# The convolution computed with tokens on partitions, later block moves, and all moves of the mixer on ScalarE's queue

## The chip, the cores and the metric

The kernel runs on one core of a Trainium2 chip, in float32. The metric is the device time of one execution, in microseconds (us). An execution under the profiler gives the trace; other executions give the times.

## The reference

One layer of a hybrid encoder, on x of 256 tokens by 2048:

```
h  = rms_norm(x);  P = h @ W_in        # 2048 x 4416: u | b | c (1024 each), c_q 768, c_kv 512, k_rope 64
yA = b * dwconv3_causal(c * u)         # three taps per channel, over tokens
yA = group_rms_norm(yA, 8 groups of 128 channels)
q  = rms_norm(c_q) @ W_uq;  kv = rms_norm(c_kv) @ W_ukv
yB = attention of 8 heads (nope 128, rope 64, v 128), block-causal in chunks of 64; per-head rms_norm
x  = x + rms_norm(concat(yA, yB) @ W_o)
x  = x + rms_norm(relu(rms_norm(x) @ W_up)^2 @ W_down)     # hidden width 8192
```

## The kernel before, in words

**Products.** Every weight matrix is streamed once from DRAM in quads: four blocks of 128 rows by up to 512 columns, 1 MB, one DMA each on SyncE's queue (SP), into a ring of 4 slots (`raw`, L605). For each half of a quad, ScalarE rounds it to a high part (L1005, `w_hi`) and VectorE subtracts to get a low part (L1305, `w_lo`). TensorE forms each product from three matmuls, hi*hi, lo*hi and hi*lo (L725 to L727), for two blocks of 128 tokens. So a half of a quad is twelve matmuls. The hi/lo ring holds four halves (`AHEAD`): ScalarE may split half h + 4 once TensorE has finished half h.

**Order.** `plan()` (L76) writes one list of steps, and every engine walks that same list in order, doing its own part of each step. An instruction that waits therefore holds back everything behind it on its engine. A step `mm` (quad, k) is one fourth of a quad on TensorE; at every odd k ScalarE and VectorE split the half that lies four further on. First come three strips of the latent columns (halves 0 to 23; the third strip is only 320 columns wide), then six strips of u, c, b, u, c, b (512 columns each, `CONV_PARTS`), then the output projection from W_o, then the MLP. A counter `sub` numbers the `mm` steps of those six strips and of W_o: strips are steps 0 to 95, W_o starts at step 96. `between(sub)` puts the mixer's other work into the list before step `sub`. In this text "step 34" is `sub` 34.

**Attention.** The head pairs p = 0 to 3 start at step 8 + 16p. Relative to that start: k and q leave PSUM, `kq_turn` at 6 (VectorE transposes 32x32 blocks into `blk`), `q_order` at 13 (ScalarE copies the moved q into `qT`, L1138), `scores` at 15 (TensorE, L909), softmax, `pv` at 22, `o_squares` at 24 (VectorE reduces, GpSimd raises to -1/2), `o_norm` at 25, `o_turn` at 26, `o_split` at 36.

**Block moves.** A turned batch in `blk` has its blocks transposed in place, but they still have to change partitions. SyncE does this in `move_batch` (L624): it waits for the turn, writes four DMAs of `blk` to a DRAM scratch `mix_rows` (L634), waits until they have landed, and reads it back with one DMA (L647). It does this between weight loads, once quad n + 4 has been requested. There are twelve such batches: two of the latents, four kq, four o, two conv.

**Convolution.** The products c*u and b of the first 512 channels are turned and moved like the others (`conv_turn` at steps 38 and 54); those of the second 512 are transposed by TensorE (`convT`, L944, four calls of four transposes). The convolution then runs with channels on partitions, on 128x256 pieces, eight in all: ScalarE applies one tap, VectorE the other two (L1520) and b. ScalarE squares, a TensorE matmul against `ones` sums over partitions (L957, eight of them), ScalarE takes the root (L1200), VectorE inverts it (L1532), applies it and writes the hi and lo parts (L1533 to L1536). These are at steps 70 + 6c and following for the first half, 98 + 4c for the second.

**Residual.** At quad `RESIDUAL_QUAD` SyncE also loads `g_post_mix` and `x_res` (L680, L681).

Of the kernel before, what the change touches and what calls it, by code (L numbers as in the profile page):

```python
# [33 lines left out]
P = 128  # L34
# [32 lines left out]
G_MIX, G_MLP, G_Q, G_KV, G_CONV, G_ATT, G_TAP = 0, 16, 32, 38, 42, 50, 58  # L67
G_ROWS = G_TAP + 3 * (CW // P)
# [4 lines left out]
CONV_PARTS = "ucb" * 2  # L73


def plan():  # L76
# [53 lines left out]
    def between(sub):  # L130
        if sub == 2:
            steps.append(("latT", 0, 0))
# [4 lines left out]
        if sub in (38, 54):  # L137
            turn("conv", sub // 54)
        for p in range(PAIRS):
# [10 lines left out]
            if at == 6:  # L150
                turn("kq", p)
            if at == 26:
                turn("o", p)
# [5 lines left out]
        for c in range(4):  # L159
            for half, t, norm in [(0, 70 + 6 * c, 8), (1, 98 + 4 * c, 5)]:  # L160
                if sub == t:
                    steps.append(("convT", half, c))
                if sub == t + 2:
                    steps.append(("conv_square", half, c))
                if sub == t + norm:
                    steps.append(("conv_norm", half, c))
# [15 lines left out]
    order = [(0, 2), (0, 3), (0, 0), (1, 2), (1, 3), (1, 0), (0, 1), (1, 1)]  # L182
# [119 lines left out]
def hybrid_block(nc, t, out):  # L302
    steps, tail, quads, batches = plan()
    BATCH = {(kind, i): n for n, (kind, i, _) in enumerate(batches)}
# [6 lines left out]
    with ExitStack() as ctx:  # L311
# [10 lines left out]
        neg_half = tensor(ctx, "neg_half", [P, 4])  # L322
# [18 lines left out]
        mean_sq = tensor(ctx, "mean_sq", [P, 8, 4])  # L341
        eps_col = tensor(ctx, "eps_col", [P, 1])
# [10 lines left out]
        with ExitStack() as mixer:  # L353
# [4 lines left out]
            rotated = tensor(mixer, "rotated", [P, TB, 2, ROPE])  # L358
            cos_t = tensor(mixer, "cos_t", [P, TB, 2 * ROPE])
            sin_t = tensor(mixer, "sin_t", [P, TB, 2 * ROPE])  # L360
            rope_c = tensor(mixer, "rope_c", [P, 2, ROPE])
            rope_s = tensor(mixer, "rope_s", [P, 2, ROPE])
# [14 lines left out]
            NCONV = 2  # L377
            conv_y = tensor(mixer, "conv_y", [P, NCONV, SEQ])
            conv_s = tensor(mixer, "conv_s", [P, NCONV, SEQ])
            conv_u = tensor(mixer, "conv_u", [P, NCONV, SEQ])  # L380
# [48 lines left out]
        convT_filled, tap_ready, conv_y_ready = sem("convT_filled"), sem("tap_ready"), sem("conv_y_ready")  # L429
        conv_sq_ready, conv_sum_done = sem("conv_sq_ready"), sem("conv_sum_done")  # L430
        conv_std_ready = sem("conv_std_ready")
# [80 lines left out]
        mix_rows = nc.dram_tensor("mix_rows", (4, BLK, 4, 8 * BLK), F32, kind="Internal").ap()  # L512
# [13 lines left out]
        def conv_landed(e):  # L526

            return as_blocks((u_sb, b_sb)[e][:, 0].rearrange("p b n -> p (b n)"))
# [52 lines left out]
        def conv_blocks(e, c):  # L581

            return conv_landed(e)[:, :, :, c].rearrange("p g b i -> p b g i")
# [3 lines left out]

        def conv_bank(half, c):
            return 7 if half == 0 else 4 + c
# [12 lines left out]
        def _(sp):  # L602
# [21 lines left out]
            def move_batch(m):  # L624

                kind, i, _ = batches[m]
                size = 4 * BLK if kind == "o" else 8 * BLK
                sp.wait_ge(blk_turned, m + 1)
                if m:

                    sp.wait_ge(blk_landed, 16 * m)
                for g in range(4):
                    src = blk[BLK * g:BLK * (g + 1)].rearrange("p q b c i -> p q (b c i)")[:, :, 0:size]
                    sp.dma_start(mix_rows[:, :, g, 0:size].rearrange("q r n -> r q n"), src).then_inc(blk_stored, 16)  # L634
                if kind == "kq":
                    sp.wait_ge(latT_lo_ready, 2)
                    if i:
                        sp.wait_ge(scores_done, 2 * i)
                elif kind == "lat" and i:
                    sp.wait_ge(latT_lo_ready, i)  # L640
                elif kind == "o":
                    sp.wait_ge(latT_lo_ready, 3)
                    sp.wait_ge(kr_ready, 4)
                    if i:
                        sp.wait_ge(oT_lo_ready, i)
                sp.wait_ge(blk_stored, 64 * (m + 1))
                sp.dma_start(landing(kind, i), mix_rows[:, :, :, 0:size].rearrange("q r g n -> (q r) g n")  # L647
                             ).then_inc(blk_landed, 16)

# [13 lines left out]
            for n in range(RAW, NQ):  # L663
# [6 lines left out]
                if n == 7:  # L670
                    sp.dma_start(ident[:], t["ident"]).then_inc(ident_landed, 16)
                    sp.dma_start(cos_t[:], t["cos"]).then_inc(tables_landed, 16)
                    sp.dma_start(sin_t[:], t["sin"]).then_inc(tables_landed, 16)
                for m, (_, _, after) in enumerate(batches):
                    if after == n:
                        move_batch(m)
                if n == RESIDUAL_QUAD:

                    sp.wait_ge(oT_lo_ready, PAIRS)
                    sp.dma_start(g_post_mix[:], t["post_mix_g"].to_broadcast([P, D])).then_inc(g_mix_landed, 16)  # L680
                    sp.dma_start(x_res[:], x_dram).then_inc(x_res_landed, 16)  # L681
# [36 lines left out]
        def _(pe):  # L718
# [50 lines left out]
            def stream(n, k, tbs=range(TB)):  # L769
# [103 lines left out]
            def step(what, a, b):  # L873
# [61 lines left out]
                elif what == "convT" and a == 1:  # L935

                    pe.wait_ge(strip_out_dve, 2)
                    pe.wait_ge(strip_out_act, 7)

                    pe.wait_ge(o_ready, PAIRS)  # L940
                    if conv_bank(a, b) == conv_bank(0, 0):

                        pe.wait_ge(conv_std_ready, 4)
                    transposes(conv_bank(a, b), [s[:, a, tb, b * P:(b + 1) * P] for s in (u_sb, b_sb)  # L944
                                                 for tb in range(TB)]).then_inc(convT_filled, 1)
                elif what == "conv_norm":

                    i = 4 * a + b
                    pe.wait_ge(ones_ready, 1)
                    pe.wait_ge(conv_sq_ready, i + 1)  # L950
                    if i == 0:

                        pe.wait_ge(probsT1_ready, PAIRS)
                    elif a == 0:

                        pe.wait_ge(conv_std_ready, b)
                    nc.tensor.matmul(ps[:, conv_bank(a, b), 0:SEQ], ones[:], conv_s[:, i % NCONV, :],  # L957
                                     start=True, stop=True).then_inc(conv_sum_done, 1)
# [39 lines left out]
        def _(act):  # L998
# [58 lines left out]
            def step(what, a, b):  # L1057
# [116 lines left out]
                elif what == "convT":  # L1174
                    i = 4 * a + b
                    if a:
                        act.wait_ge(convT_filled, b + 1)
                    else:
                        act.wait_ge(blk_landed, landed(("conv", 1)))
                    if i >= NCONV:  # L1180

                        act.wait_ge(convT_ready, i - NCONV + 1)

                    tap = G_TAP + 2 * 8 + i
                    if a:
                        nc.scalar.activation(conv_y[:, i % NCONV], ps[:, conv_bank(a, b), 0:SEQ], ACT.Copy,
                                             scale=gains[:, tap:tap + 1]).then_inc(tap_ready, 1)
                    else:
                        nc.scalar.activation(by_block(conv_u[:, i % NCONV]), conv_blocks(0, b), ACT.Copy)
                        nc.scalar.activation(by_block(conv_y[:, i % NCONV]), conv_blocks(0, b), ACT.Copy,  # L1190
                                             scale=gains[:, tap:tap + 1]).then_inc(tap_ready, 1)
                elif what == "conv_square":
                    i = 4 * a + b
                    act.wait_ge(conv_y_ready, i + 1)
                    nc.scalar.activation(conv_s[:, i % NCONV], conv_y[:, i % NCONV],
# [636 lines left out]
```

## Time and profile before

| | us |
|---|---|
| median of 3 runs | 1068.28 (1066.87 to 1068.4) |
| the profiled execution's own time | 1067.39 |
| span of its trace, from the first to the last instruction | 1065.6 |
| TensorE busy | 1053.6 |
| VectorE busy | 695.2 |
| ScalarE busy | 515.9 |
| GpSimd busy | 80.7 |

Lines name the engines PE (TensorE matmul), PEld (its weight load), DVE (VectorE), ACT (ScalarE), POOL (GpSimd) and SP (SyncE); a "q" behind the name is that engine's sequencer, as where it issues a DMA. Busy times are sums over the span. A matmul's end is modelled, so the distance between the starts of two matmuls, not the length of one, tells what one costs.

### The profile page before, as it was taken

What the parts mean: (1) busy time and instruction counts of PE and PEld (TensorE: products, weight loads), DVE (VectorE), ACT (ScalarE), POOL (GpSimd) and SP (SyncE); (2) the same over time, 40 slices, a digit from 0 to 9 for tenths busy, and PEclk for the clock granted to TensorE, in tenths of its full rate; (3) what the DMA queues carried; (4) which work ended last, traced back from release to release, by engine and by line L of the source; (5) the groups of instructions that cost most, each with busy time, mean ns of one, the idle gap of its engine ahead of it and who ended that gap; (6) DMA issues with size and microseconds to landing.
All of it is one profiled execution on the core that took longest, in us unless ns stands there. A gap on an engine that the chain in (4) does not pass through costs nothing.

```text
span 1065.6 us, 13494 instructions
## 1 busy us (share of the span) xinstructions
PE 1053.6 (99%) x4794; PEld 877.0 (82%) x4794; DVE 695.2 (65%) x785; ACT 515.9 (48%) x666; POOL 80.7 (8%) x94
## 2 busy tenths in 40 slices
PE   9999999999999999999999999999999999999996
PEld 7898888888888788888888888888888888888885
DVE  6475566679975876575575665756657656565666
ACT  7575545565544664444444444444444444444443
POOL 0011022110000310000000000000000000000003
PEclk9999999999999999999999999999999999999998
DMA  9786667864586465776666756666576665676562
GB/s 345 261 300 218 201 184 272 271 221 151 204 307 198 125 212 157 237 226 197 209 184 212 231 172 232 196 199 212 170 236 216 203 211 159 220 232 190 181 242 79
DMA packets 125619, 225.78 MB, mean 212 GB/s; under 512 B 8464, under 2 KB 30096, under 8 KB 124816
## 3 DMA queue, kind: packets, MB, share of 16 engines
q1 hardware_dynamic: 125152, 224.89, 64.7%
q10 hardware_dynamic: 432, 0.44, 0.1%
q8 instruction: 21, 0.34, 0.1%
q14 instruction: 14, 0.11, 0.0%
HBM read 210.08 MB, written 7.34 MB: 204 GB/s over the span
## 4 chain that ended last, share of the span: by engine, by line
PE 85%; issue 11%; DVE 2%; POOL 1%; DMA 1%; ACT 0%; SPq 0%; DVEq 0%; POOLq 0%; ACTq 0%
PE ps L725 28%; PE ps L727 28%; PE ps L726 28%; DMA raw<-in_w_in 1%; PE ps L748 1%; POOL acc L1666 0%; DVE w_lo L1305 0%; PE ps L909 0%; PE ps L914 0%; POOL x_res L1777 0%; POOL x_res L1751 0%; ACT w_hi L1005 0%; SPq L656 0%; DVE conv_s L1532 0%; DVEq L311 0%
## 5 line engine op out<-in xcount | busy, mean ns | idle before, releaser
L1305 DVE TENSOR_TENSOR w_lo<-raw,w_hi 128x1024 fp32r<-128x1024 f32 (+2 forms) x382 | 465.2, 1226 | 318.9 <-ACT w_hi L1005 316.8
L1005 ACT ACTIVATE w_hi<-raw 128x1024 fp32r<-128x1024 f32 (+2 forms) x382 | 395.8, 1038 | 460.7 <-PE ps L727 456.3
L725 PE MATMUL ps<-w_hi,xT_hi 128*128 128x512 f32 (+1 forms) x792 | 308.5, 390 | 0.6 <-DVE xT_lo L1406 0.5
L727 PE MATMUL ps<-w_lo,xT_hi 128*128 128x512 f32 (+1 forms) x792 | 305.9, 386 | 0.0
L726 PE MATMUL ps<-w_hi,xT_lo 128*128 128x512 f32 (+1 forms) x792 | 305.8, 386 | 0.0
L725 PE MATMUL ps<-w_hi,yT_hi 128*128 128x512 f32 x672 | 263.1, 391 | 0.0
L727 PE MATMUL ps<-w_lo,yT_hi 128*128 128x512 f32 x672 | 261.6, 389 | 0.0
L726 PE MATMUL ps<-w_hi,yT_lo 128*128 128x512 f32 x672 | 261.4, 389 | 0.0
L725 PEld LDWEIGHTS ps<-w_hi,xT_hi 128*128 128x128 f32 x792 | 148.7, 188 | 31.9 <-issue 2.0
L727 PEld LDWEIGHTS ps<-w_lo,xT_hi 128*128 128x128 f32 x792 | 148.6, 188 | 30.0
L726 PEld LDWEIGHTS ps<-w_hi,xT_lo 128*128 128x128 f32 x792 | 148.8, 188 | 28.7
L727 PEld LDWEIGHTS ps<-w_lo,yT_hi 128*128 128x128 f32 x672 | 126.1, 188 | 26.5
L726 PEld LDWEIGHTS ps<-w_hi,yT_lo 128*128 128x128 f32 x672 | 126.2, 188 | 26.1
L725 PEld LDWEIGHTS ps<-w_hi,yT_hi 128*128 128x128 f32 x672 | 126.1, 188 | 25.9
L1379 DVE TENSOR_TENSOR acc<-acc,ps 128x1024 f32<-128x1024 f32 x58 | 70.8, 1220 | 18.4 <-PE ps L727 17.5
L1685 POOL TENSOR_TENSOR a_sb<-a_sb 128x1024 f32<-128x1024 f32 x16 | 30.3, 1895 | 583.0 <-ACT a_sb L1035 583.0
L1035 ACT ACTIVATE a_sb<-ps,rstd_x 128x512 f32<-128x512 f32 x32 | 20.2, 683 | 19.9 <-PE ps L727 19.9
L1325 DVE TENSOR_TENSOR yT_lo<-aT_raw,yT_hi 128x512 fp32r<-128x512 f32 x32 | 20.6, 683 | 0.0
L1350 DVE STREAM_TRANSPOSE a_blk<-a_sb 128x512 f32<-128x512 f32 x30 | 19.5, 687 | 0.0
L1044 ACT ACTIVATE yT_hi<-aT_raw 128x512 fp32r<-128x512 f32 x32 | 18.2, 615 | 1.5 <-DVE aT_raw L1360 1.5
L1672 POOL TENSOR_TENSOR rope_c<-q_sb,cos_t 128x128 f32<-128x128 f32 x8 | 8.6, 1073 | 114.6 <-ACT q_sb L1129 114.3
L727 PE MATMUL ps<-w_lo,cqT_hi 128*128 128x384 f32 x48 | 16.1, 335 | 0.0
(155 smaller groups left out, 425.3 us busy)
## 6 DMA issues: line engine op xcount, KB each, us to landing
raw<-in_w_up SPq DMA_DIRECT2D x64, 1024.0 KB, 5.5
raw<-in_w_down SPq DMA_DIRECT2D x64, 1024.0 KB, 5.3
raw<-in_w_in SPq DMA_DIRECT2D x28, 1024.0 KB, 6.0
raw<-in_w_o SPq DMA_DIRECT2D x16, 1024.0 KB, 5.0
aT_raw<-a_blk SPq DMA_DIRECT2D x240, 32.0 KB, 1.9
raw<-in_w_uq SPq DMA_DIRECT2D x8, 576.0 KB, 4.9
mix_rows<-blk SPq DMA_DIRECT2D x32, 128.0 KB, 2.4
raw<-in_w_ukv SPq DMA_DIRECT2D x4, 1024.0 KB, 5.3
```

The source lines that it names most:

```text
L725: nc.tensor.matmul(dst, x_hi, hi, start=first, stop=False)
L726: nc.tensor.matmul(dst, x_lo, hi, start=False, stop=False)
L727: mm = nc.tensor.matmul(dst, x_hi, lo, start=False, stop=last)
L748: mm = nc.tensor.transpose(ps[:, bank, i * P:(i + 1) * P], src, ident[:])
L1005: nc.scalar.activation(w_hi[:, slot, 0:size], raw[:, raw_slot, first:first + size], ACT.Copy).then_inc(hi_ready, 1)
L1035: ins = nc.scalar.activation(a_sb[:, tb], ps[:, bank + tb], ACT.Relu, scale=rstd_x2[:, tb:tb + 1])
L1044: ins = nc.scalar.activation(turned(yT_hi, at, tb), blocked(tb), ACT.Copy)
L1305: nc.vector.tensor_tensor(w_lo[:, slot, 0:size], raw[:, raw_slot, first:first + size], f32(w_hi[:, slot, 0:size]), ALU.subtract).then_inc( ...
L1325: ins = nc.vector.tensor_tensor(turned(yT_lo, at, tb), blocked(tb), f32(turned(yT_hi, at, tb)), ALU.subtract)
L1350: ins = nc.vector.transpose(a_blk[:, :, tb].rearrange("p q c i -> p c q i"), a_sb[:, tb].rearrange("p (c q i) -> p c q i", c=4, q=4))
L1379: nc.vector.tensor_tensor(m, m, ps[:, bank:bank + 2], ALU.add).then_inc(acc_added, 1)
L1685: nc.gpsimd.tensor_tensor(a, a, a, ALU.mult).then_inc(a_ready, 1)
```

## The change

1. The convolution stays with tokens on partitions. The product c*u (256 x 512 of a half) is stored to a second DRAM scratch `conv_rows` with two zero rows ahead of it, and read back twice, shifted by one and two tokens (`u_store`, `u_back1`, `u_back2`, ScalarE's queue). The taps are loaded as rows broadcast to all partitions (`taps`). VectorE does six operations on 128x1024 (`conv_mix` 0 to 5), ScalarE one square, VectorE one reduction, GpSimd the power -1/2, VectorE one scaling; then both halves are turned and moved as blocks (`conv_turn`) and split by both engines (`conv_split`). TensorE's transposes (`convT`) and its sums against `ones` are gone.
2. Steps: the turns of conv are at 89 and 104 instead of 38 and 54; the splits at 105 and 115.
3. All twelve moves are issued by ScalarE (`move_store`, `move_read`). The store is in the list one step after the turn, and the read 4 (kq), 5 (o) or 6 (conv) steps after it. `mix_rows` has two halves, used in turns.
4. W_o's first two strips take row block 0 later: (0,2) (0,3) (1,2) (1,3) (0,0) (1,0) (0,1) (1,1).
5. `x_res` is loaded four quads after `g_post_mix`, and `g_post_mix` also waits for `ss_c_ready`.

```diff
-    def turn(kind, i):
-        batches.append((kind, i, len(quads) + 4))
+    def turn(kind, i, at=None):
+        batches.append((kind, i))
         steps.append((kind + "_turn", i, len(batches) - 1))
+        if at is not None:
+            moves.setdefault(at + 1, []).append(("move_store", len(batches) - 1, 0))
+            moves.setdefault(at + MOVE[kind], []).append(("move_read", len(batches) - 1, 0))
...
+                for b, when in enumerate([((1, 2, 3), (1, 3, 3)), ((2, 0, 3), (2, 2, 2))]):
+                    if (s, q, k) in when:
+                        steps.append((("move_store", "move_read")[when.index((s, q, k))], b, 0))
...
     def between(sub):
+        steps.extend(moves.pop(sub, []))
...
-        if sub in (38, 54):
-            turn("conv", sub // 54)
...
             if at == 6:
-                turn("kq", p)
+                turn("kq", p, sub)
             if at == 26:
-                turn("o", p)
+                turn("o", p, sub)
...
+        for h in range(2):
+            for when, what in [(4, "taps"), (34, "u_store"), (40, "u_back1"), (67, "u_back2")] if h == 0 else [
+                    (79, "taps"), (83, "u_store"), (88, "u_back1"), (88, "u_back2")]:
+                if sub == when:
+                    steps.append((what, h, 0))
+            for op, when in enumerate([(50, 56, 58, 76, 77, 83), (87, 91, 92, 94, 95, 98)][h]):
+                if sub == when:
+                    steps.append(("conv_mix", h, op))
+            for when, what in [[(84, "conv_square"), (86, "conv_stats"), (89, "conv_scale"), (105, "conv_split")],
+                               [(99, "conv_square"), (101, "conv_stats"), (104, "conv_scale"), (115, "conv_split")]][h]:
+                if sub == when:
+                    steps.append((what, h, 0))
+            if sub == (89, 104)[h]:
+                turn("conv", h, sub)
...
-            def move_batch(m):
...
+                if n == 9:
+                    sp.wait_ge(zeros_ready, 1)
+                    sp.dma_start(conv_rows[:, 0:2].rearrange("h r n -> r h n"),
+                                 blk[0:2].rearrange("p q b c i -> p (q b c i)").rearrange("p (h n) -> p h n", h=2)
+                                 ).then_inc(zeros_stored, 16)
...
-                            pe.wait_ge(convT_ready, 4 * z["q"] + 4)
+                            pe.wait_ge(convT_ready, z["q"] + 1)
...
+                elif what == "move_store":
+                    kind, i = batches[a]
+                    size = 4 * BLK if kind == "o" else 8 * BLK
+                    act.wait_ge(blk_turned, a + 1)
+                    for g in range(4):
+                        src = blk[BLK * g:BLK * (g + 1)].rearrange("p q b c i -> p q (b c i)")[:, :, 0:size]
+                        act.dma_start(mix_rows[a % 2, :, :, g, 0:size].rearrange("q r n -> r q n"), src
+                                      ).then_inc(blk_stored, 16)
+                elif what == "move_read":
...
+                    act.wait_ge(blk_stored, 64 * (a + 1))
+                    act.dma_start(landing(kind, i), mix_rows[a % 2, :, :, :, 0:size].rearrange("q r g n -> (q r) g n")
+                                  ).then_inc(blk_landed, 16)
...
+                elif what == "conv_split":
+                    act.wait_ge(blk_landed, landed(("conv", a)))
+                    for c in range(4):
+                        k = 4 * a + c
+                        ins = nc.scalar.activation(by_block(yT_hi[:, k]),
+                                                   conv_landed(a)[:, :, :, c].rearrange("p g b i -> p b g i"),
+                                                   ACT.Copy, scale=gains[:, G_CONV + k:G_CONV + k + 1])
+                    ins.then_inc(convT_hi_ready, 1)
...
+                elif what == "conv_mix":
+                    u = u_sb[:, a]
+                    dst, other, op = [(u, tap(2), ALU.mult), (shifted[0], tap(1), ALU.mult), (u, shifted[0], ALU.add),
+                                      (shifted[1], tap(0), ALU.mult), (u, shifted[1], ALU.add),
+                                      (u, b_sb[:, a], ALU.mult)][b]
...
+                    nc.vector.tensor_tensor(dst, dst, other, op).then_inc(conv_mixed, 1)
```

## Rows read from the trace of the kernel before

**Rows 1.** The page: busy time of each engine, share of the span, instructions.
```profile
PE 1053.6 (99%) x4794; PEld 877.0 (82%) x4794; DVE 695.2 (65%) x785; ACT 515.9 (48%) x666; POOL 80.7 (8%) x94
```

**Rows 2.** TensorE's waits from 15 to 1045 us: total, times, longest.
```profile
PE ps L748 <- POOL x_res L1751: 0.5, 1, 0.5
```

**Rows 3.** Busy time in a stretch: length, then busy (count) of each engine, clock, DMA.
```profile
247.00:300.00 53.00, 53.00 (x243) 43.76 (x242) 50.70 (x71) 27.67 (x41) 0.81 (x1) 1.00 0.64 223
```

**Rows 4.** Timeline of TensorE (start, length, engine, line) around a transpose and a sum.
```profile
272.41 0.39 PE L727 MATMUL ps<-w_lo,yT_hi 128*128 128x512 f32 x1
273.31 0.39 PE L726 MATMUL ps<-w_hi,yT_lo 128*128 128x512 f32 x1
...
274.23 0.39 PE L727 MATMUL ps<-w_lo,yT_hi 128*128 128x512 f32 x1
275.11 0.39 PE L726 MATMUL ps<-w_hi,yT_lo 128*128 128x512 f32 x1
```

**Rows 5.** Timeline of TensorE: the scores of pairs 1, 2 and 3.
```profile
147.24 1.47 PE L909 MATMUL ps<-kqT,lat 128*128 128x128 f32 x8
...
185.44 1.47 PE L909 MATMUL ps<-kqT,lat 128*128 128x128 f32 x8
...
223.65 1.47 PE L909 MATMUL ps<-kqT,lat 128*128 128x128 f32 x8
```

**Rows 6.** Timeline of VectorE around pair 1's turn of kq and pair 0's of o.
```profile
137.26 0.67 DVE L1334 STREAM_TRANSPOSE blk<-q_sb 128x512 f32<-128x512 f32 x1
138.75 1.23 DVE L1305 TENSOR_TENSOR w_lo<-raw,w_hi 128x1024 fp32r<-128x1024 f32 x1 [0.83 <-ACT w_hi L1005]
...
143.31 0.69 DVE L1502 TENSOR_TENSOR o_sb<-o_sb,rstd_o 128x512 f32<-128x512 f32 x1 [1.42 <-POOL rstd_o L1658]
...
145.38 0.70 DVE L1334 STREAM_TRANSPOSE blk<-o_sb 128x512 f32<-128x512 f32 x1
```

**Rows 7.** Timeline of ScalarE in the same stretch.
```profile
137.66 1.06 ACT L1005 ACTIVATE w_hi<-raw 128x1024 fp32r<-128x1024 f32 x1 [3.02 <-PE ps L727]
...
143.35 1.06 ACT L1005 ACTIVATE w_hi<-raw 128x1024 fp32r<-128x1024 f32 x1 [1.66 <-PE ps L727]
145.14 0.72 ACT L1138 ACTIVATE lat<-kqT 128x256 f32<-128x256 f32 x2 [0.72 <-DMA kqT<-mix_rows]
```

**Rows 8.** Timelines of SyncE's and ScalarE's queues: issues of a move, and one on ScalarE.
```profile
137.95 1.78 SPq L634 DMA_DIRECT2D mix_rows<-blk  x4
141.71 0.34 SPq L647 DMA_DIRECT2D kqT<-mix_rows  x1
...
1.18 0.45 ACTq L1050 DMA_DIRECT2D xT_raw<-in_xT  x1
```

**Rows 9.** Timeline of VectorE: the turns of o of pairs 1 and 2.
```profile
182.28 0.70 DVE L1334 STREAM_TRANSPOSE blk<-o_sb 128x512 f32<-128x512 f32 x1
...
220.48 0.70 DVE L1334 STREAM_TRANSPOSE blk<-o_sb 128x512 f32<-128x512 f32 x1
```

**Rows 10.** Timelines of ScalarE, VectorE and TensorE in the last latent strip.
```profile
55.99 1.70 ACT L1106 ACTIVATE cqT_hi<-kqT,gains 128x256 fp32r<-128x256 f32 x4
...
54.44 1.30 DVE L1334 STREAM_TRANSPOSE blk<-lat 128x512 f32<-128x512 f32 x2
...
57.72 2.19 DVE L1339 SCALAR_TENSOR_TENSOR cqT_lo<-kqT,gains,cqT_hi 128x128 fp32r<-128x128 f32 x8 [0.78 <-ACT cqT_hi L1106]
...
61.21 0.31 PE L726 MATMUL ps<-w_hi,xT_lo 128*128 128x320 f32 x1
```

**Rows 11.** All DMAs that touch the scratch: issue to landing.
```profile
DMA to landing us min/median/max: 1.7/2.7/6.3
```

**Rows 12.** Timelines of TensorE and ScalarE: two neighbouring matmuls, and a table load.
```profile
248.98 0.39 PE L726 MATMUL ps<-w_hi,xT_lo 128*128 128x512 f32 x1
249.21 0.39 PE L727 MATMUL ps<-w_lo,xT_hi 128*128 128x512 f32 x1
...
237.53 1.28 ACT L1200 ACT_TABLE_LOAD   x1
```

More of the change, by code:

```diff
@@ L179, in plan @@
         steps.append(("conv_out", i, n))
-    order = [(0, 2), (0, 3), (0, 0), (1, 2), (1, 3), (1, 0), (0, 1), (1, 1)]
+    order = [(s, q) for qs in ((2, 3), (0,), (1,)) for s in (0, 1) for q in qs]
     order += [(s, q) for s in (2, 3) for q in (2, 3, 0, 1)]
@@ L622, in move_blocks @@
                                      ).then_inc(aT_landed, 16)
-            def move_batch(m):
[L626 to L648, printed above, removed]
             def load_x(tb):
@@ L934, in step @@
                     mm.then_inc(pv_done, 1)
[L935 to L958, printed above, removed]
                 elif what == "hT":
@@ L1173, in step @@
                                rstd_x).then_inc(strip_out_act, 1)
-                elif what == "convT":
-                    i = 4 * a + b
-                    if a:
-                        act.wait_ge(convT_filled, b + 1)
-                    else:
[L1179 to L1191, printed above, removed]
-                elif what == "conv_square":
-                    i = 4 * a + b
-                    act.wait_ge(conv_y_ready, i + 1)
-                    nc.scalar.activation(conv_s[:, i % NCONV], conv_y[:, i % NCONV],
-                                         ACT.Square).then_inc(conv_sq_ready, 1)
-                elif what == "conv_norm":
-                    i = 4 * a + b
-                    act.wait_ge(conv_sum_done, i + 1)
-                    nc.scalar.activation(conv_s[:, i % NCONV], ps[:, conv_bank(a, b), 0:SEQ], ACT.Sqrt,
-                                         scale=1.0 / P, bias=eps_col[:, 0:1]).then_inc(conv_std_ready, 1)
@@ new lines, in step @@
+                elif what == "move_store":
[7 more added lines that the diff above has]
+                elif what == "move_read":
+                    kind, i = batches[a]
+                    size = 4 * BLK if kind == "o" else 8 * BLK
+                    if kind == "kq":
+                        act.wait_ge(latT_lo_ready, 2)
+                        if i:
+                            act.wait_ge(scores_done, 2 * i)
+                    elif kind == "lat" and i:
+                        act.wait_ge(latT_lo_ready, i)
+                    elif kind == "o":
+                        act.wait_ge(latT_lo_ready, 3)
+                        act.wait_ge(kr_ready, 4)
+                        if i:
+                            act.wait_ge(oT_lo_ready, i)
+                    if a:
+                        act.wait_ge(blk_landed, 16 * a)
+                    act.wait_ge(blk_stored, 64 * (a + 1))
+                    act.dma_start(landing(kind, i), mix_rows[a % 2, :, :, :, 0:size].rearrange("q r g n -> (q r) g n")
+                                  ).then_inc(blk_landed, 16)
+                elif what == "taps":
+                    if a:
+                        act.wait_ge(conv_mixed, 4)
+                    for k in range(3):
+                        act.dma_start(conv_w[:, k], t["conv_w"][0, k:k + 1, a * W:(a + 1) * W].to_broadcast([P, W])
+                                      ).then_inc(conv_w_landed, 16)
+                elif what == "u_store":
+                    act.wait_ge(strip_out_dve, a + 1)
+                    act.dma_start(conv_rows[a, 2:2 + SEQ].rearrange("(b p) n -> p b n", p=P), u_sb[:, a]
+                                  ).then_inc(u_stored, 16)
+                elif what in ("u_back1", "u_back2"):
+                    back = int(what[-1])
+                    act.wait_ge(u_stored, 16 * (a + 1))
+                    act.wait_ge(zeros_stored, 16)
+                    if a:
+                        act.wait_ge(ss_c_ready, a)
+                    elif back == 1:
+                        act.wait_ge(latT_lo_ready, 3)
+                        act.wait_ge(krT_filled, 1)
+                    else:
+                        act.wait_ge(q_rope_ready, 4 * PAIRS)
+                        act.wait_ge(qrT_filled, PAIRS)
+                    act.dma_start(shifted[back - 1], conv_rows[a, 2 - back:2 - back + SEQ].rearrange(
+                        "(b p) n -> p b n", p=P)).then_inc(u_shifted[back - 1], 16)
+                elif what == "conv_square":
+                    act.wait_ge(conv_mixed, 6 * a + 6)
+                    nc.scalar.activation(shifted[0], u_sb[:, a], ACT.Square).then_inc(conv_sq_ready, 1)
+                    if a == 0:
+                        nc.scalar.activation(std_m[:], ones[:, 0:TB], ACT.Sqrt)
+                elif what == "conv_split":
[6 more added lines that the diff above has]
+                    ins.then_inc(convT_hi_ready, 1)
@@ L1423, in step @@
                 elif what == "conv_turn":
-                    if a == 0:
-                        dve.wait_ge(strip_out_dve, 1)
-                    else:
-                        dve.wait_ge(strip_out_act, 5)
-                    src = (u_sb, b_sb)[a]
-                    turn_batch(b, [src[:, 0, tb].rearrange("p (c q i) -> p c q i", c=4, q=4) for tb in range(TB)])
+                    dve.wait_ge(conv_scaled, a + 1)
+                    turn_batch(b, [u_sb[:, a, tb].rearrange("p (c q i) -> p c q i", c=4, q=4) for tb in range(TB)])
                 elif what == "lat_split":
```

131 lines of the change are left out of this document (67 added, 64 removed).

## The prediction, made before the changed kernel had run

> **What bounds the kernel now.** I read the busy times first [rows 1]: TensorE works 1053.6 of the span's 1065.6 us, no other engine more than two thirds of it. Then who waits on TensorE's side [rows 2]: between 15 and 1045 us it waited 0.5 us in all. So each matmul taken out shortens the kernel by its own cost, and each microsecond for which TensorE has to wait lengthens it. An engine beside it costs nothing until it is later than the ring of four halves allows. Two neighbouring matmuls start 0.23 us apart [rows 12], so a half (twelve) passes in about 2.72 us and a step in 1.36. VectorE is the engine closest to being late: in the convolution's stretch it is busy 50.7 of 53 us [rows 3].
>
> **What TensorE sheds.** From a product to the next but one takes 0.90 us with a group of four transposes in between, and 0.88 us with a sum against `ones` [rows 4]; two plain distances are 0.46. So a group of transposes costs 0.44 and a sum 0.42 us. There are four groups and eight sums: 4 x 0.44 + 8 x 0.42 = 5.1 us. All of it is on the path, since TensorE never rests there.
>
> **Other work that goes, comes or moves, and is hidden.** The weight loads leave SyncE earlier, as no move stands between them any more; since TensorE does not wait for loads now [rows 2], that is worth 0. The zero rows (8 KB) go out with quad 9, long before the first turn needs `blk`: 0. The loads of taps and the shifts by DRAM have 4 to 27 steps each before their users: 0 to 1 us. The new order of W_o's quads only gives the convolution more time. `g_post_mix` and `x_res` are needed tens of microseconds later: 0.
>
> **The moves on ScalarE: attention.** This is the part that decides. SyncE could wait for a turn without hurting anyone; ScalarE has the hi splits and `q_order` queued behind the waiting store. A store is four issues, 1.78 us on SyncE, and one issue on ScalarE's queue took 0.45 [rows 8], so I take 1.77 us per store; from below, if they overlap other work, 1.2.
>
> Pair 1, on before's clock. The turn of kq ends at 137.26 + 0.67 = 137.93 [rows 6]. ScalarE would start its next split at 137.66 [rows 7], but the store (step 31) stands ahead of it and waits for the turn: 137.93 + 1.77 = 139.70. The split is 2.0 us late, so VectorE's part of it (138.75 [rows 6]) is too, and behind that on VectorE come the reduction, GpSimd's power, `o_norm` (143.31) and the turn of pair 0's o, which ended at 145.38 + 0.70 = 146.08 [rows 6] and now ends at 148.1. At step 35 the store of this o waits on ScalarE for exactly that turn: 148.1 + 1.77 = 149.9. Behind it come the split of step 35 (1.06, at 143.35 before) and only then `q_order` (0.72, at 145.14 before) [rows 7]: 151.6. TensorE reaches the scores at 147.24 [rows 5] and needs `qT`. Wait: 4.4 us.
>
> Pair 2 has no product c*u on VectorE in the chain; before, its turn of o ended at 182.98 [rows 9]. 182.98 + 2.05 + 1.77 + 1.06 + 0.72 = 188.6 against 185.44 [rows 5]: 3.1 us. Pair 3: 220.48 + 0.70 = 221.18 [rows 9], the same terms and one more issue (`u_back2`, 0.43): 227.2 against 223.65 [rows 5]: 3.6 us. Pair 0 has no store of o ahead of its `q_order`; the read goes out about when it did: 0 (at most 2.4, below). Together 11.1 us. From below, without the 2.0 us of lateness and with stores of 1.2 us: 1.8 + 0.5 + 0.9, about 3 us.
>
> **The latents.** The narrow third strip leaves little time. The second turn (54.44 + 1.30 before [rows 10]) becomes about 1.0 us later since the read of the first batch, which waits for its stores, stands before ScalarE's output of the second strip. The second store (step after that turn) then waits until 56.7 and issues until 58.5; `lat_split` follows (1.70), at 55.99 before [rows 10], now 58.5 to 60.2; VectorE's part (2.19 [rows 10]) ends at 62.4 and the lo split behind it at 63.2. TensorE wants that half at 61.2 [rows 10]. Wait: 2.0 us (0.5 to 4).
>
> **The convolution's new place.** From step 83 to 104 VectorE has 11 lo splits and 7 mixes of 128x1024, 2 reductions and 2 scalings of the same size, 4 turns of 128x512 and the split of pair 3's o: 22 x 1.15 + 4 x 0.63 + 1.1 = 28.9 us (a 1024-wide operation is 1.23 long, a turn 0.70 [rows 6], and neighbours overlap by 0.08). TensorE passes these 22 steps in 29.9 us. That would fit, but VectorE also waits for others there: for ScalarE while it issues the store of pair 3's o and `u_store` (2.2 us), while it squares and loads the root's table (1.06 + 1.28 [rows 12]), 0.7 at the store of conv 0, 2.1 at the second square, 1.2 for GpSimd's power. 28.9 + 8.5 = 37.4 against 29.9 and some 3.5 us in hand: TensorE waits about 4 us, in pieces at several halves. Then one chain at steps 104 and 105: scale and turn (2.4), the store on ScalarE (1.77), `conv_split` of the first half on ScalarE (4 pieces, 1.7 as in [rows 10]) and on VectorE (2.1, [rows 10]), and only then the lo split of that step (1.15): 9.1 us from the moment at which VectorE gets to the scaling. I find that moment 4.5 us before TensorE wants step 112's half and `convT_ready`: 4.6 us more. The second half has five steps to spare: 0. Together 8.7 us; from below, if VectorE finds gaps that I count as waits, 2; from above 14.
>
> **Sum.** -5.1 + 11.1 + 2.0 + 8.7 = +16.7 us. From the profiled execution's own 1067.4 us this gives 1084; the median of the runs shown is 0.9 higher, so I say 1085.
>
> **A rule weighed.** The moves now share the 16 DMA engines with weight loads from another queue, instead of standing in line with them. Before, a DMA of the scratch landed 2.7 us after its issue, at most 6.3 [rows 11]. The Trainium skill (DMA: Bandwidth & Descriptors, "Issuing engines are not separate DMA queues") says that DMAs started by several engines run on the same 16 engines and interleave, and that a second issuer saves only issue time, usually small. By it no transfer gets quicker, which agrees with my 0 for the loads; taken as "issue time is small" it would also make the stores on ScalarE nearly free, and the sum would drop by the eight stores of 1.77 that stand in it, about 14 us, to 1070, the upper end of the absorbed case below; the row of 1.78 us speaks against that [rows 8].
>
> **The rivals.**
> - *Waits mostly absorbed*: the same mechanism at its lower ends: -5.1 + 3 + 0.5 + 2 = about 0, or 1068; with the latents at 2 and the convolution at 5 us +5, or 1072. I put the case at 1071. For it: ScalarE is busy only 48% and each engine has slack of several us in the ring. Against it: the order of the list is fixed, and `q_order` cannot pass the store.
> - *TensorE's work alone decides* (the other side): no wait reaches it, for which the turns would have to end some 4 us earlier against the scores than the rows show. 1067.4 - 5.1 = 1062. It decides where `q_order` ends before TensorE gets to the scores in all four pairs. For it: ScalarE has 52% idle time and VectorE is busy 65% [rows 1], so each has room on the whole. Against it: rows 5 to 9.
> - *Moves land late*: with reads or stores at 6.3 instead of 2.7 to 3.3 [rows 11], pair 0's `q_order` is 2.4 us late, the latents 3 more, the second conv move 3: +8 on the forecast, 1093. For it: the loads no longer leave a gap for the moves. Against it: a 512 KB read with a load just behind it took 3.4 us before.
> - *The change does nothing that can be told*: gains and waits cancel, within 0.2% (2 us, about what a measurement can tell from no change): 1068.
>
> **How the numbers follow.** Forecast 0.60; absorbed 0.15 (a third of it within 0.2% or just above); late landings 0.15; TensorE alone 0.06; cancelled 0.04. The range reaches from the absorbed case, 1071, to the late landings, 1095. Faster by over 0.2%: 0.07; within: 0.05; slower: 0.88.
>
> **What would show each step.** In the changed trace: no `ones` sums and no transposes of `u_sb`; TensorE idle before the scores of pairs 1, 2 and 3 by 3 to 4.5 us each, released by ScalarE's `q_order`, and none before pair 0's; ScalarE's stores of o issued right after VectorE's turn; idle of about 2 us near 61 us behind VectorE's lo split; several waits of under 1 us behind lo splits in steps 88 to 104 and one of over 4 at step 112. I am wrong if TensorE has no idle before the scores, if a store on ScalarE takes well under 1 us, or if VectorE reaches step 104 more than 9 us ahead of TensorE's step 112.

## The result and the profile after

The changed kernel takes 1100.13 us (median of 4 runs, 1098.55 to 1101.99) against 1067.91 on the same chip (1066.87 to 1068.4): ratio 1.0303, 95% interval 1.029 to 1.0316. So it is 32 us slower. I had said 1085, range 1071 to 1095: the direction was right, the size was not. The profiled execution has a span of 1096.8 us at a granted clock of 0.988, against 1065.6 at 0.997.

First the page of the changed kernel: busy times, and the clock in 40 slices. It answers to [rows 1].

```profile
PE 1059.2 (97%) x4762; PEld 877.5 (80%) x4762; DVE 686.2 (63%) x761; ACT 508.6 (46%) x649; POOL 88.7 (8%) x98
...
PEclk9999999999989999999999999999999999999998
```

TensorE has 32 matmul instructions fewer and is busy 5.6 us longer. Two things are to be seen in that: work went, and what is left runs slower somewhere. Slice 12, from 302 to 329 us, is the only one in the middle with a lower clock digit. VectorE and ScalarE do less than before, and so no engine has become the bound; the time is in waits. The view of waits on TensorE (total, times, longest), where [rows 2] had the 0.5 us of `x_res` alone:

```profile
PE ps L716 <- DVE w_lo L1313: 13.8, 7, 6.0
PE ps L900 <- issue: 11.7, 3, 4.6
PE ps L849 <- POOL ones L1704: 1.9, 1, 1.9
...
PE ps L739 <- POOL x_res L1773: 0.5, 1, 0.5
```

"Issue" as the releaser of the scores (L900) means only that the profile shows nothing that TensorE waited for. What did is told by ScalarE's timeline around pair 1's scores. Its columns are start, length, engine, line, operation; "ACTq" is an issue on ScalarE's queue.

```profile
144.49 1.78 ACTq L1147 DMA_DIRECT2D mix_rows<-blk  x4
146.37 2.01 ACT L972 ACTIVATE w_hi<-raw 128x1024 fp32r<-128x1024 f32 x2 [5.19 <-issue]
...
154.83 1.81 ACTq L1147 DMA_DIRECT2D mix_rows<-blk  x4
156.75 1.06 ACT L972 ACTIVATE w_hi<-raw 128x1024 fp32r<-128x1024 f32 x1 [8.37 <-DMA mix_rows<-blk]
157.71 0.70 ACT L1105 ACTIVATE lat<-kqT 128x256 f32<-128x256 f32 x2
```

and VectorE's in the same stretch, which answers to [rows 6]:

```profile
143.79 0.67 DVE L1344 STREAM_TRANSPOSE blk<-q_sb 128x512 f32<-128x512 f32 x1
147.47 1.22 DVE L1313 TENSOR_TENSOR w_lo<-raw,w_hi 128x1024 fp32r<-128x1024 f32 x1 [3.00 <-ACT w_hi L972]
...
154.10 0.70 DVE L1344 STREAM_TRANSPOSE blk<-o_sb 128x512 f32<-128x512 f32 x1
```

The turn of o ends at 154.80 and the store is issued from 154.83 on, the very moment. Behind it come the split and `q_order` (L1105), whose last piece ends at 158.41. TensorE starts the scores at 158.52:

```profile
158.52 2.30 PE L900 MATMUL ps<-kqT,lat 128*128 128x128 f32 x8 [4.59 <-issue]
160.75 1.65 PE L905 MATMUL ps<-krT,qrT_sb 64*128 64x128 f32 x8
...
201.79 1.55 PE L900 MATMUL ps<-kqT,lat 128*128 128x128 f32 x8 [3.25 <-issue]
203.27 0.93 PE L905 MATMUL ps<-krT,qrT_sb 64*128 64x128 f32 x8
...
244.11 2.55 PE L900 MATMUL ps<-kqT,lat 128*128 128x128 f32 x8 [3.88 <-issue]
246.59 1.55 PE L905 MATMUL ps<-krT,qrT_sb 64*128 64x128 f32 x8
```

Read the lengths as well as the pauses. The same eight matmul instructions of scores and eight of the rotated part take 2.41 us from first start to last end in pair 2 (201.79 to 204.20), but 3.88 in pair 1 and 4.03 in pair 3. The view by windows (start:end, length, busy time of PE, PEld, DVE, ACT, POOL, then the granted clock, DMA share, GB/s) says why:

```profile
60.00:64.00 4.00, 3.88 (x16) 3.88 (x17) 2.11 (x4) 2.45 (x7) 0.00 (x0) 0.57 0.49 119
...
158.00:163.00 5.00, 4.48 (x18) 3.02 (x19) 2.78 (x6) 1.36 (x3) 0.00 (x0) 0.66 0.64 213
201.00:205.00 4.00, 3.21 (x20) 2.39 (x21) 3.15 (x6) 1.64 (x4) 0.00 (x0) 1.00 0.49 135
244.00:249.00 5.00, 4.89 (x20) 3.42 (x21) 2.63 (x6) 0.95 (x2) 0.00 (x0) 0.66 0.90 290
288.00:293.00 5.00, 4.59 (x13) 3.62 (x14) 4.08 (x8) 3.68 (x6) 0.00 (x0) 0.66 0.58 161
...
318.00:324.00 6.00, 5.43 (x15) 4.33 (x16) 3.92 (x4) 1.27 (x2) 0.00 (x0) 0.58 0.52 183
```

After five of the larger pauses, TensorE ran for some microseconds on the lower level (1.2 GHz) before the granted clock was back at 2.4. After pair 2's it did not. Nor did it after the pause of 2.42 us at 68 us. The cost can be read off the starts of matmuls, here at the biggest pause:

```profile
312.22 0.39 PE L718 MATMUL ps<-w_lo,yT_hi 128*128 128x512 f32 x1
318.57 0.80 PE L716 MATMUL ps<-w_hi,yT_hi 128*128 128x512 f32 x1 [5.96 <-DVE w_lo L1313]
319.16 0.63 PE L717 MATMUL ps<-w_hi,yT_lo 128*128 128x512 f32 x1
319.58 0.63 PE L718 MATMUL ps<-w_lo,yT_hi 128*128 128x512 f32 x1
...
323.00 0.40 PE L717 MATMUL ps<-w_hi,yT_lo 128*128 128x512 f32 x1
323.24 0.40 PE L718 MATMUL ps<-w_lo,yT_hi 128*128 128x512 f32 x1
```

Neighbours are 0.43 apart instead of the 0.23 of [rows 12]. Eleven distances (318.57 to 323.24) take 4.67 us where 11 x 0.227 = 2.50 would do: 2.2 us lost. The same sum gives 1.6 us from 60.12 to 63.48, 1.7 from 288.41 to 292.41, and the scores 1.5 and 1.6: 8.6 us in all.

**The account.** The pauses of 0.15 us and more before the latents, the scores and the tail of the convolution add up to 2.31 + 2.42, 4.59 + 3.25 + 3.88 and 0.15 + 0.41 + 0.34 + 2.19 + 5.96 = 25.5 us. By distances of starts they are some 0.16 longer each (6.35 - 0.23 = 6.12 for the one shown as 5.96): 27.1. With the lower clock 8.6, and 5.1 for the matmuls that went, the sum is 27.1 + 8.6 - 5.1 = +30.6 us; the spans differ by 31.2. So 0.6 us has no place. The kernel's start does not fill it: GpSimd clears `blk` first and lets TensorE begin at 1.86 us instead of 1.01, but a wait of 0.88 us for a hi split a little later is gone, and the first matmul of L716 starts at 12.43 us, where its like (L725) started at 12.77 before, so 0.3 us earlier. With that, some 0.9 us is open.

### The profile page after: what moved, and what is told of

It reads as the page before. It is cut to its first block, busy times and chain, and to the rows that moved or that the text cites. A ratio compares the mean times of both kernels' runs of the same rounds, so it can differ in the third digit from the quotient of the medians.

```text
span 1096.8 us, 13395 instructions
## 1 busy us (share of the span) xinstructions
PE 1059.2 (97%) x4762; PEld 877.5 (80%) x4762; DVE 686.2 (63%) x761; ACT 508.6 (46%) x649; POOL 88.7 (8%) x98
## 4 chain that ended last, share of the span: by engine, by line
PE 79%; issue 10%; DVE 3%; DMA 3%; POOL 2%; ACT 2%; ACTq 1%; SPq 0%; DVEq 0%; POOLq 0%
PE ps L716 26%; PE ps L718 26%; PE ps L717 26%; DMA raw<-in_w_in 2%; DVE w_lo L1313 1%; DMA mix_rows<-blk 1%; ACT w_hi L972 1%; PE ps L900 1%; ACTq L1147 1%; PE ps L739 1%; POOL acc L1682 0%; POOL rstd_c L1674 0%; PE ps L905 0%; DVE u_sb L1537 0%; DVE blk L1344 0%
## 5 line engine op out<-in xcount | busy, mean ns | idle before, releaser
L716 PE MATMUL ps<-w_hi,xT_hi 128*128 128x512 f32 (+1 forms) x792 | 309.5, 391 | 6.2 <-DVE w_lo L1313 5.6
L716 PE MATMUL ps<-w_hi,yT_hi 128*128 128x512 f32 x672 | 263.7, 392 | 8.2 <-DVE w_lo L1313 8.1
L716 PEld LDWEIGHTS ps<-w_hi,xT_hi 128*128 128x128 f32 x792 | 149.5, 189 | 39.7 <-DVE w_lo L1313 8.5
L716 PEld LDWEIGHTS ps<-w_hi,yT_hi 128*128 128x128 f32 x672 | 127.1, 189 | 36.1 <-DVE w_lo L1313 9.7
L900 PE MATMUL ps<-kqT,lat 128*128 128x128 f32 (+1 forms) x32 | 7.9, 401 | 11.7 <-issue 11.7
L1688 POOL TENSOR_TENSOR rope<-q_sb,rope 128x128 f32<-128x128 f32 x8 | 8.6, 1073 | 120.2 <-ACT q_sb L1096 119.9
```

What stands on the lines that cost most here:

```text
L716: nc.tensor.matmul(dst, x_hi, hi, start=first, stop=False)
L900: nc.tensor.matmul(ps[:, (6, 7)[h], cols], qT[:, tb, h], kT, start=tb == 0, stop=False, skip_group_check=True)
```

## The experiments

Eight kernels, each timed beside the kernel before on the same chip (1067.5 to 1067.6 us).

**1. All moves back on SyncE, the convolution as changed.**

```diff
-            moves.setdefault(at + 1, []).append(("move_store", len(batches) - 1, 0))
-            moves.setdefault(at + MOVE[kind], []).append(("move_read", len(batches) - 1, 0))
+            pass
...
+                for m, (_, _, after) in enumerate(batches):
+                    if after == n:
+                        move_batch(m)
```

> The changed kernel, but all twelve moves back on SyncE's queue, where they stood before (after quad n + 4 has been requested); the convolution, its steps and the two halves of the scratch stay. Theory (ScalarE in order: what is queued behind a store that waits for its turn is late): TensorE's pauses before the scores of pairs 1 to 3 (12 us), the two in the third latent strip (5) and the half-clock stretches behind three of them (4.9) go, and the tail's pauses shrink as no store stands ahead of the hi splits there: 1100 - 22 = 1078 or less. Rival (the convolution's own work on VectorE makes the kernel slow, wherever the moves are issued): the pauses before the scores stay above 1 us each and the time stays above 1090. Rival (the pauses come from slow landings, since moves and loads share the DMA engines): on SyncE the same bytes move, so the pauses stay.

Measured: 1070.08 us, ratio 1.0019 [1.0009, 1.003], lower than the 1078 that I had named as the most. 30 of the 32 us are gone with this one edit. TensorE's waits in it:

```profile
PE ps L744 <- DVE w_lo L1341: 4.5, 3, 2.2
PE ps L877 <- POOL ones L1732: 1.9, 1, 1.9
...
PE ps L928 <- issue: 0.2, 1, 0.2
```

The scores wait 0.2 us in all instead of 11.7, the latents not at all; three pauses of the convolution's tail stay (1.75, 0.52 and 2.25 us). The loads of weights stand in one queue with the moves again and nothing waits for them.

**2. The kernel before, with nothing changed but the moves: ScalarE's queue, two halves of the scratch.**

```diff
+MOVE = {"kq": 4, "o": 5, "conv": 6}
...
-                for m, (_, _, after) in enumerate(batches):
-                    if after == n:
-                        move_batch(m)
...
+                elif what == "move_store":
```

> The kernel before, with only the moves put on ScalarE's queue, with the same distances to their turns (store one step later, read 4, 5 or 6 steps after the turn). Theory: the pauses of the latents and of the scores come as in the changed kernel, 17 us and about 5 us at half clock, and none at step 112: 1068 + 22 = 1090. If the moves were harmless and the new convolution the cause, 1068 within 2 us.

Measured: 1092.62 us, ratio 1.0227 [1.021, 1.0244]: 25 us for the moves alone, with TensorE's work untouched. Its waits:

```profile
PE ps L890 <- issue: 11.1, 3, 4.6
PE ps L706 <- DVE w_lo L1314: 5.6, 4, 3.5
PE ps L717 <- ACT w_hi L1047: 1.4, 1, 1.4
```

The three pauses before the scores are those of the changed kernel (4.56, 3.25, 3.33 against 4.59, 3.25, 3.88). Experiments 1 and 2 together say that the moves carry the loss, from either side: taken out of the changed kernel they give back 30 us, put into the old one they cost 25. The 5 us between the two belong to neither alone: the pauses of the convolution's tail are 9.1 us with both, 4.5 in experiment 1 and 0.9 here.

**3. Only the store of o later: four steps after its turn instead of one, behind `q_order`.**

```diff
-            moves.setdefault(at + 1, []).append(("move_store", len(batches) - 1, 0))
-            moves.setdefault(at + MOVE[kind], []).append(("move_read", len(batches) - 1, 0))
+            late = 3 if kind == "o" else 0
+            moves.setdefault(at + 1 + late, []).append(("move_store", len(batches) - 1, 0))
+            moves.setdefault(at + MOVE[kind] + late - late // 3, []).append(("move_read", len(batches) - 1, 0))
```

> The changed kernel, with the store of o four steps after its turn instead of one (behind the next pair's q_order on ScalarE) and its read two steps later than now. Theory: q_order no longer waits for the turn of o, so the pauses before the scores of pairs 1 to 3 fall from 3.3 to 4.6 us to under 0.5 each, and the half clock behind two of them goes: 1100 - 11.7 - 3.3 = 1085. Rival (q_order is late because the moved kq lands late): pauses stay, 1100.

Measured: 1083.0 us, ratio 1.014 [1.0123, 1.0157]. No pause before any score is left, and from 100 to 260 us the clock is full:

```profile
100.00:260.00 160.00, 159.36 (x790) 134.48 (x790) 101.68 (x160) 76.87 (x126) 27.18 (x44) 1.00 0.69 223
```

17 us for the stores of o, put further down a list: 11.7 of pauses, 0.5 of their starts, 3.1 of clock, which is 15.3. The spans of the two traces differ by 14.2, as the profiled execution of this kernel was the slowest of its four, so the other 1.8 lies within the scatter of executions. The stores of o still cost ScalarE 1.8 to 2.8 us each. It is where they stand, ahead of `q_order`, that hurt.

**4. The pauses kept, but TensorE kept busy in them.** Fourteen matmuls of 128x128 on `ones` ahead of the scores of pairs 1, 2 and 3; their result is used by nobody. Two waits stand ahead of them, for the place in PSUM that they write.

```diff
+                    if p:
+                        pe.wait_ge(o_ready, p)
+                        pe.wait_ge(probsT1_ready, p)
+                        for _ in range(14):
+                            nc.tensor.matmul(ps[:, 6, 0:P], ones[:], ones[:], start=True, stop=True)
```

> The changed kernel, with 14 matmuls against ones on TensorE (about 3.1 us) in the pauses before the scores of pairs 1, 2 and 3. Nothing is computed with them. Theory (the scores of pairs 1 and 3 took 3.8 and 4.0 us instead of 2.3 since the granted clock falls after a pause): with TensorE busy in the pause the clock stays at 1.0 there, the scores take 2.3 us in all pairs, and the kernel gets 3.3 us faster: 1097, though it does more. Rival (they are slow because of DMA traffic or because of the wait itself): the scores stay slow and the time stays at 1100.

Measured: 1097.12 us, ratio 1.0269 [1.0252, 1.0286]: about 3 us faster than the changed kernel, as the theory of the clock said (two of the three pairs had lost 1.5 and 1.6). Pair 1 of this kernel (the trace counts two instructions for each of the fourteen matmuls):

```profile
156.30 3.29 PE L890 MATMUL ps<-ones 128*128 128x128 f32 x28
161.06 1.55 PE L905 MATMUL ps<-kqT,lat 128*128 128x128 f32 x8 [1.48 <-issue]
162.54 0.93 PE L910 MATMUL ps<-krT,qrT_sb 64*128 64x128 f32 x8
```

The wait is as long (3.29 of filling and 1.48 of rest against 4.59), yet the sixteen matmul instructions take 2.41 us instead of 3.88, and the stretch from 100 to 260 us has a clock of 1.00 where it was 0.98. Pair 2 of the changed kernel kept its clock without any filling, so one trace of each would prove little. But four kernels here have these pauses unfilled (the changed one, experiments 2, 5 and 6), and 10 of their 12 pauses were followed by the lower level; of the three filled ones none was. So the slow matmuls came with the idle time ahead of them, and not from the operands or from DMAs beside them. The intervals of this kernel and of the changed one all but touch (they end at 1.0286 and begin at 1.029), so the size, 3 us, is less sure than the cause.

**5. `conv_split` of the first half three steps earlier (102 instead of 105), all else as changed.**

```diff
-            for when, what in [[(84, "conv_square"), (86, "conv_stats"), (89, "conv_scale"), (105, "conv_split")],
+            for when, what in [[(84, "conv_square"), (86, "conv_stats"), (89, "conv_scale"), (102, "conv_split")],
```

> The changed kernel, with conv_split of the first half at step 102 instead of 105, so ahead of the second half's scaling, turn and store. Theory (the pause of 6.0 us at step 112 is one chain: scale, turn, four issues, eight split pieces, lo split): 1.7 us of hi pieces and 2.1 us of lo pieces leave it and fall into VectorE's idle time behind GpSimd's power; the store stays. The pause falls to 2 to 3 us: 1100 - 3.5 = 1096.5. Rival (VectorE is simply full there, so the order is of no account): the pause only moves to another step, 1100.

Measured: 1099.01 us, ratio 1.0298 [1.028, 1.0315]: not to be told from the changed kernel. The pause at step 112 fell from 5.96 to 3.97 us and no more, and three small ones came up ahead of it (0.18, 0.31, 0.51). I expected 2 to 3 us at that place and 1096.5 in all: a miss in both. The chain that is left is the scaling, the turns, the store on ScalarE (until 315.9), and behind it the hi and the lo split of that step; the split that I moved was only part of it.

**6. Only the two moves of the latents on SyncE.**

```diff
+                for m, (kind, _, after) in enumerate(batches):
+                    if after == n and kind == "lat":
+                        move_batch(m)
```

> The changed kernel, with the two moves of the latents alone back on SyncE's queue. Theory: the two pauses near 58 and 65 us (4.7 us) and the half clock behind the first (1.6) go, everything later stays: 1100 - 6.3 = 1094. Rival (the pauses in the third latent strip come from the weight loads' new timing): they stay, 1100.

Measured: 1093.32 us, ratio 1.0248 [1.0232, 1.0263]: 6.8 us less than the changed kernel, for 4.7 of pauses, 0.3 of their starts and 1.6 of clock, 6.6. TensorE is busy all of the 25 us from 50 on:

```profile
50.00:75.00 25.00, 25.00 (x149) 23.02 (x148) 17.19 (x31) 18.84 (x34) 3.60 (x9) 1.00 0.82 284
```

**7. A version to keep: moves on SyncE, and the convolution spread out.** The first half's last mixes, square, statistics, scaling, turn and split come 2 to 6 steps earlier, the second half's scaling and turn one later.

```diff
-            for op, when in enumerate([(50, 56, 58, 76, 77, 83), (87, 91, 92, 94, 95, 98)][h]):
+            for op, when in enumerate([(50, 56, 58, 72, 75, 77), (87, 91, 92, 94, 95, 98)][h]):
...
-            for when, what in [[(84, "conv_square"), (86, "conv_stats"), (89, "conv_scale"), (105, "conv_split")],
-                               [(99, "conv_square"), (101, "conv_stats"), (104, "conv_scale"), (115, "conv_split")]][h]:
+            for when, what in [[(79, "conv_square"), (81, "conv_stats"), (86, "conv_scale"), (102, "conv_split")],
+                               [(99, "conv_square"), (101, "conv_stats"), (105, "conv_scale"), (115, "conv_split")]][h]:
...
-            if sub == (89, 104)[h]:
+            if sub == (86, 105)[h]:
```

> The kernel of e1 (new convolution, moves on SyncE), with steps moved into VectorE's idle times: mixes 3 to 5 of the first half at 72, 75, 77, its square at 79, sums at 81, scaling and turn at 86, its split at 102; the second half's scaling and turn at 105. Theory (the 2.5 us that e1 is behind the kernel before are 4.5 us of pauses and 1.7 us at half clock in the tail, against 5.1 us of matmuls saved): with the pauses gone it is 1070 - 6 = 1064, faster than the kernel before by 3.5 us. If VectorE's sum of work in steps 83 to 112 is what counts and not its order, 1068 to 1070.

Measured over five rounds: 1063.62 us, ratio 0.9965 [0.9951, 0.9979]. It is faster than both kernels, by 4 us than the one before. The stretch in which the changed kernel was worst, at full clock and without a rest, and all that TensorE waited for:

```profile
310.00:340.00 30.00, 30.00 (x135) 24.83 (x134) 15.96 (x16) 13.39 (x17) 0.00 (x0) 1.00 0.72 241
```

```profile
PE ps L877 <- POOL ones L1732: 1.9, 1, 1.9
PE ps L928 <- DMA kqT<-mix_rows: 0.8, 1, 0.8
...
PE ps L928 <- issue: 0.3, 1, 0.3
```

Of the 5.1 us that TensorE sheds, 4 arrive; 1.1 is lost again before the scores: 0.8 in pair 3, for a read of the scratch, and 0.3 in pair 1.

**8. Experiment 1 with `conv_split` of the first half at 102.**

```diff
-            for when, what in [[(84, "conv_square"), (86, "conv_stats"), (89, "conv_scale"), (105, "conv_split")],
+            for when, what in [[(84, "conv_square"), (86, "conv_stats"), (89, "conv_scale"), (102, "conv_split")],
```

> The kernel of e1 with only conv_split of the first half at step 102. Theory: of its three tail pauses (1.75, 0.52, 2.25 us) the last goes, with the half clock of 1.7 us behind it: 1070 - 3.5 = 1066.5. Rival (VectorE full): the time stays at 1070.

Measured: 1068.11 us, ratio 1.0002 [0.9992, 1.0012]. I had expected 1066.5, and 1070 by the rival; it lies between. The last pause of experiment 1 went from 2.25 to 0.58 and its slow matmuls with it; the other two stayed (1.75, 0.52), and 1.2 us of waiting for a read of the scratch before pair 3's scores came up, as did 1.1 for a hi split in the first 9 us, where the kernel before waits 0.9. In the medians the edit buys 2.0 us with the moves on SyncE and 1.1 with them on ScalarE (5). The intervals of experiments 1 and 8 overlap a little, those of the changed kernel and 5 almost wholly, and so the difference between the two gains is not shown. That it comes from the store on ScalarE, which stands between scaling and split there, is argued and not tested.

## Why the prediction was right and wrong

- *TensorE sheds 5.1 us.* Right: 32 matmuls fewer, and experiment 7, in which hardly a wait is left, is 4 us faster with 1.1 of waits.
- *Scores, 4.4, 3.1 and 3.6, none before pair 0's: 11.1.* Right in place, cause and size: 4.59, 3.25, 3.88, and none in pair 0. The turn of pair 0's o, which I had 0.9 us after the moment at which TensorE wants pair 1's scores, ended 0.87 us after it (154.80, against 158.52 - 4.59 = 153.93). Experiment 3 takes the cause away and the pauses go.
- *Latents, 2.0 in one pause.* Too small: 2.31 and 2.42. I took 1.77 us for the first store, from [rows 8]; its four issues took 3.29. And I let the first read delay ScalarE by about 1 us; it waited 5.0 for the stores to land:

```profile
47.59 3.29 ACTq L1147 DMA_DIRECT2D mix_rows<-blk  x4
...
56.88 0.34 ACTq L1167 DMA_DIRECT2D kqT<-mix_rows  x1
57.32 1.26 ACT L987 ACTIVATE lat<-ps,rstd_x 128x512 f32<-128x512 f32 x2 [4.98 <-DMA mix_rows<-blk]
...
63.15 1.71 ACT L1073 ACTIVATE cqT_hi<-kqT,gains 128x256 fp32r<-128x256 f32 x4 [1.52 <-issue]
```

  The stores landed some 6 us after the last issue, which is the upper end of [rows 11], not its middle. The DMA share was 0.96 from 56 to 60 us; that this delayed the stores is not shown, since no run took the loads away. Other executions divide it differently (1.22, 0.39 and 3.50 in experiment 2), so the place is sensitive, but the sum was about 5 us in both. This is my rival of moves that land late, true at one of its three places: at the scores and the conv moves TensorE did not wait for a landing, and experiment 1 has no pause at the latents. It does not account for the result, as it had priced these landings at 1093 in all.
- *The convolution's tail, about 4 in pieces and 4.6 at step 112: 8.7.* The sum was right (0.15 + 0.41 + 0.34 + 2.19 and 5.96: 9.1), partly by errors that cancel. GpSimd's statistics of 8 columns took 3.59 us where I had 1.2 from rows with 4 columns, and ScalarE's store, split and the lo split come as one chain as I had said:

```profile
305.28 1.10 POOL L1671 TENSOR_SCALAR mean_sq<-ss_c 128x8 f32<-128x8 f32 x1 [20.62 <-DVE ss_c L1540]
306.46 2.49 POOL L1674 TENSOR_TENSOR rstd_c<-mean_sq,neg_half 128x8 f32<-128x8 f32 x1
```

```profile
308.98 1.23 DVE L1545 TENSOR_TENSOR u_sb<-u_sb,rstd_c 128x1024 f32<-128x1024 f32 x1 [1.53 <-POOL rstd_c L1674]
310.24 1.30 DVE L1344 STREAM_TRANSPOSE blk<-u_sb 128x512 f32<-128x512 f32 x2
315.19 2.19 DVE L1349 SCALAR_TENSOR_TENSOR yT_lo<-b_sb,gains,yT_hi 128x128 fp32r<-128x128 f32 x8 [3.64 <-ACT yT_hi L1206]
317.29 4.63 DVE L1313 TENSOR_TENSOR w_lo<-raw,w_hi 128x1024 fp32r<-128x1024 f32 x4
```

  From 308.98 to the end of the first lo split at 318.5 are 9.5 us, which I had as 9.1. But VectorE got to the scaling only 3.6 us before TensorE wanted that half (at 312.6), where I had 4.5.
- *The term that was missing: the clock.* This is the step that failed. I priced a pause as its own length; all through the prediction a microsecond of waiting cost a microsecond. The five pauses above cost another 8.6, the scores alone 3.1 on their 11.7; without them the kernel would stand at some 1091.5. Experiment 4 shows the cause. The trace of the kernel before could not have given the price, since no long pause in it has matmuls behind it, but it had the sign: TensorE's last matmul ends at 1056.6 us, and the granted clock reads 1.00 until 1060 and 0.50 from 1060.5 on, without anything running. I put the term at nothing and had no reason for it. With this term, 2.7 more at the latents, 1.0 at scores and tail, and 1.6 for the starts behind pauses, 16.7 becomes 30.6.
- *The rule that issue time is small* (the Trainium skill, DMA: Bandwidth & Descriptors, "Issuing engines are not separate DMA queues") I had weighed as a sum of 1070 for free stores. The trace stands against a reading of it as "a move costs its engine nothing": stores held ScalarE 1.78, 1.81 and 3.29 us. What decided was neither. The same page of the Trainium skill says under "Anatomy of one DMA — SWDGE (gpsimd) path" that DMA engines do not wait on semaphores, and that such a wait is done by the issuing sequencer before dispatch. The trace agrees: with the store of o waiting for its turn, ScalarE computed nothing from 148.38 to 156.75 us, and it had `q_order` next (experiments 1 and 3).

Not settled: why pair 2's pause of 3.25 us and the 2.42 us pause at 68 kept the clock, while the 2.19 at 288 and the 2.31 at 60 lost it. The traces of the experiments say that the length of a pause does not decide it: pair 2's pause of 3.25 us kept the clock in the changed kernel and in experiment 6 and lost it in 2 and 5, and the pause of 2.19 us lost it in the changed kernel and in 3, 4 and 6 and kept it in 5. So a part of the 8.6 us is luck of the one execution that was traced. Open too are the 0.9 us of the account, and the parts of the change that no kernel took out alone (the order of W_o's strips, the later load of `x_res`); TensorE's wait for `x_res` is 0.5 us in both kernels.

## What to carry to other kernels

Here a DMA cost the engine that issued it 0.45 us or more of issue time, and everything queued behind the wait that stood ahead of it came late as well: before a move goes to a compute engine's queue, write down what is next on that engine and who wants it when. Work that must be waited for belongs on a queue with nothing urgent behind it (30 us here), or in the list behind the urgent operation (17 us for the stores of o). And in a kernel whose TensorE never rests, price a pause above its length, as a chance and not as a sure cost: here 25.5 us of idle cost 8.6 more in slow matmuls.

## What the runs showed that I had not expected

- Pauses of 2.2 to 6 us on TensorE were followed in five of seven cases of over 2 us by 3.4 to 4.7 us at the lower clock level, and in 24 of 29 such cases over the traces of all kernels here; filling the pauses with matmuls of no use avoided it (3.88 to 2.41 us for the same sixteen instructions), and was itself faster than resting, by 3 us in the medians.
- GpSimd on 128x8 took 1.10 us for the scaled mean and 2.49 for the power -1/2; on 128x4 the same two took 0.20 and 1.02: twice the columns, 5.5 and 2.4 times the time.
- Four issues of one store took 1.78 to 1.94 us in most places of the changed kernel and 3.29 in the first, near 48 us, on the same queue (3.32 and 2.55 at that place in experiments 2 and 3).
